# Softmax attention: row-sum reciprocals spread by a DRAM store and a repeating load, and four PSUM banks for transposes

## The reference, cut to what matters

```python
def one_block(args):                      # forgetting attention, 128 queries
    s = jnp.einsum('bhqd,bhkd->bhqk', qb, kh).astype(jnp.float32) * scale
    s = s + cb[..., :, None] - c[..., None, :]
    p = jax.nn.softmax(jnp.where(mask, s, -jnp.inf), axis=-1)
    return jnp.einsum('bhqk,bhkd->bhqd', p.astype(vh.dtype), vh)
...
def memory_attention(q, mk, mv):
    s = jnp.einsum('bthd,bmhd->bhtm', q, mk).astype(jnp.float32) * (D ** -0.5)
    p = jax.nn.softmax(s, axis=-1)
    o = jnp.einsum('bhtm,bmhd->bthd', p.astype(mv.dtype), mv)
...
o_fox = o_fox.astype(x.dtype) * jax.nn.silu(f_gate)
```

## Time and profile before

| | us |
|---|---|
| time before, median of 3 runs | 1407.98 (1406.86 to 1414.48) |
| profiled execution, its own time | 1410.44 |
| its span | 1408.6 |
| PE busy in the span | 1281.9 (91%) |
| DVE, ACT, POOL busy | 671.4, 547.2, 416.0 |
| memory attention | about 717 to 840 |
| forgetting attention | about 840 to 1217 |

### The profile page before, as it was taken

How to read it: one execution, slowest core, us unless ns; L and a number is a source line. 1 busy time by engine, 2 the same in 40 slices (tenths; PEclk the granted TensorE clock), 3 DMA queues, 4 the chain that set the end, 5 groups by cost and what they waited for, 6 DMA issues and landing times. The chain is left out here.

```text
span 1408.6 us, 20363 instructions
## 1 busy us (share of the span) xinstructions
PE 1281.9 (91%) x6624; PEld 1038.4 (74%) x6624; DVE 671.4 (48%) x1622; ACT 547.2 (39%) x1131; POOL 416.0 (30%) x464
## 2 busy tenths in 40 slices
PE   5898999999999999999976759998999999599997
PEld 4887867888777777788854546786777777478886
DVE  4564414200545544500045547887887888322222
ACT  3563214012222222211145646776777777310100
POOL 5222431021444444430005682223223412300000
PEclk9999999999999999999977888999999999799999
DMA  6454213222544454331156535134341611465453
GB/s 212 150 156 127 76 59 114 74 82 83 157 150 153 149 157 154 125 105 64 46 150 186 133 74 137 51 112 93 89 137 29 154 24 24 146 210 193 180 205 121
DMA packets 118350, 170.40 MB, mean 121 GB/s; under 512 B 11908, under 2 KB 74628, under 8 KB 116404
## 3 DMA queue, kind: packets, MB, share of 16 engines
q1 hardware_dynamic: 115768, 160.65, 37.9%
q10 hardware_dynamic: 2304, 8.39, 1.5%
q0 software_dynamic: 192, 0.33, 0.2%
HBM read 103.19 MB, written 66.13 MB: 120 GB/s over the span
## 5 line engine op out<-in xcount | busy, mean ns | idle before, releaser
L834 PE MATMUL cg_cps<-h_T,tok_slot 128*128 128x512 f32 x2112 | 493.7, 393 | 3.4 <-POOL tok_slot L1074 3.4
L834 PEld LDWEIGHTS cg_cps<-h_T,tok_slot 128*128 128x128 f32 x2112 | 396.4, 189 | 89.2 <-POOL tok_slot L1074 4.3
L1719 PE MATMUL out_yps<-out_w,out_mix 128*128 128x512 f32 x768 | 177.4, 393 | 18.3 <-DMA out_mix<-scr_mix 17.3
L1719 PEld LDWEIGHTS out_yps<-out_w,out_mix 128*128 128x128 f32 x768 | 145.8, 190 | 49.8 <-DMA out_mix<-scr_mix 17.5
L1559 DVE TENSOR_SCALAR_CACHE_REDUCE fox_prob<-fox_sps 128x512 f32<-128x512 f32 (+2 forms) x240 | 142.1, 607 | 37.8 <-PE fox_sps L1444 34.9
L1521 ACT ACTIVATE fox_pT<-fox_tps 128x512 fp32r<-128x512 f32 x240 | 124.6, 531 | 90.1 <-PE fox_tps L1454 87.6
L1570 DVE TENSOR_TENSOR fox_pT<-fox_tps,fox_pT 128x512 fp32r<-128x512 f32 x240 | 141.7, 605 | 21.6 <-ACT fox_pT L1521 20.9
L1454 PE MATMUL fox_tps<-all_ident,fox_prob 128*128 128x128 f32 x816 | 135.1, 278 | 15.4 <-ACT fox_prob L1513 8.5
L1467 PE MATMUL fox_ops<-fox_pT,fox_v 128*128 128x512 f32 x480 | 137.3, 376 | 0.0
L1454 PEld LDWEIGHTS fox_tps<-all_ident,fox_prob 128*128 128x128 f32 x816 | 100.4, 141 | 45.5 <-ACT fox_prob L1513 11.6
L1439 PE MATMUL fox_sps<-fox_ka,fox_qa 128*128 128x512 f32 (+2 forms) x240 | 107.4, 448 | 17.4 <-PEq L1376 14.0
(11 more groups left out here) (187 smaller groups left out, 1676.3 us busy)
## 6 DMA issues: line engine op xcount, KB each, us to landing
scr_split<-cg_stage SPq DMA_DIRECT2D x64, 256.0 KB, 2.8
out_mix<-scr_mix SPq DMA_DIRECT2D x32, 512.0 KB, 4.2
tok_xin<-in_w_cols SPq DMA_DIRECT2D x22, 512.0 KB, 4.4
tok_xin<-in_x SPq DMA_DIRECT2D x16, 512.0 KB, 3.9
scr_gates<-cg_stage SPq DMA_DIRECT2D x32, 256.0 KB, 2.4
out_x<-in_x SPq DMA_DIRECT2D x16, 512.0 KB, 6.1
out<-out_o ACTq DMA_DIRECT2D x16, 512.0 KB, 5.0
scr_fox_v<-tok_vst SPq DMA_DIRECT2D x16, 384.0 KB, 2.9
```

What stands on the lines that cost most here:

```text
L834: mm = nc.tensor.matmul(cps[u % 2][:, :], w[j % 2][a_][:, kk, :], hT[b_][:, kk, c * CH:(c + 1) * CH], start=(kk == 0 and r == 0), stop=(kk ...
L1719: mm = nc.tensor.matmul(yps[s][:, c, :], mix[s][a][:, kk, :], w[b][:, kk, c * CH:(c + 1) * CH], start=(kk == 0 and n == 0), stop=(kk == MI ...
```

## The change

The reciprocals no longer pass through PE and PSUM. After the first block of turn t, ACT issues a DMA that stores `rinv` to a DRAM row of 512 floats (`scr.inv`, one of two), each float to its own place in the order of the queries. SP then issues a load that reads this row 64 times, once for each partition of `scale`. ACT's store waits until the gate multiply of turn t - 2 is done, and so does SP's load; SP issues load_scale(t + 1) before it waits for the output of turn t, and the first, load_scale(0, 0), behind the list of first loads. The bank `rps` becomes a fourth `tps`, and PE's transposes may run one block further ahead of DVE. POOL's gate multiply waits for the load instead of ACT's copy. Its place in POOL's list stays.

```diff
@@ -55,6 +55,7 @@
         self.lr = dram("scr_lr", [GLA_R, T], F32)
         self.gla_b = dram("scr_gla_b", [64 + GLA_DK, 2, T], F32)
         self.crow = dram("scr_crow", [4, FOX_H, T], F32)
+        self.inv = dram("scr_inv", [2, CH], F32)
         self.mix = dram("scr_mix", [2, TT, P, MIX_T, P], F32)
 
 
@@ -1331,14 +1332,17 @@
         o = [k.sb(f"o{b}", [DH, CH]) for b in range(2)]
         om = [[k.sb(f"om{b}{i}", [DH, CH], F32R) for i in (HI, LO)] for b in range(2)]
         sps = [k.ps(f"sps{b}", [P, CH]) for b in range(2)]
-        tps = [k.ps(f"tps{b}", [P, CH]) for b in range(3)]
+        TPS = 4
+        tps = [k.ps(f"tps{b}", [P, CH]) for b in range(TPS)]
         ops = [k.ps(f"ops{b}", [P, CH]) for b in range(2)]
-        rps = k.ps("rps", [P, CH])
         names = ("pool_goes gate_scaled gate_loaded0 gate_loaded1 scored negated maxed expd transposed pt_hi pt_lo "
-                 "weighed inverted spread low_done added scaled gated o_hi o_lo stored0 stored1 sp_goes").split()
+                 "weighed inverted inv_stored0 inv_stored1 low_done added scale_loaded0 scale_loaded1 gated o_hi o_lo stored0 stored1 "
+                 "sp_goes act_goes").split()
         (pool_goes, gate_scaled, gate_loaded0, gate_loaded1, scored, negated, maxed, expd, transposed, pt_hi, pt_lo,
-         weighed, inverted, spread, low_done, added, scaled, gated, o_hi, o_lo, stored0, stored1, sp_goes) = map(k.sem, names)
+         weighed, inverted, inv_stored0, inv_stored1, low_done, added, scale_loaded0, scale_loaded1, gated, o_hi, o_lo, stored0,
+         stored1, sp_goes, act_goes) = map(k.sem, names)
         gate_loaded, stored = (gate_loaded0, gate_loaded1), (stored0, stored1)
+        scale_loaded, inv_stored = (scale_loaded0, scale_loaded1), (inv_stored0, inv_stored1)
 
         n_scores = sum(len(list(score_units(*t))) for t in turns)
         n_keys = sum(len(list(key_units(*t))) for t in turns)
@@ -1391,9 +1395,20 @@
                 for stage in next_stages:
                     stage.first_loads(sp)
 
+                def load_scale(r, t):
+                    b = t % 2
+                    sp.wait_ge(inv_stored[b], 16 * (r * (n_turns // 2) + t // 2 + 1))
+                    sp.sem_inc(sp_goes, 1)
+                    sp.wait_ge(gate_scaled, r * n_turns + max(t - 1, 0))
+                    sp.sem_inc(sp_goes, 1)
+                    sp.dma_start(scale[b][:, :], scr.inv[b].partition_broadcast(DH)).then_inc(scale_loaded[b], 16)
+
                 def round_(r, last):
                     for t, (e, g) in enumerate(turns):
-
+                        if t + 1 < n_turns:
+                            load_scale(r, t + 1)
+                        elif not last:
+                            load_scale(r + 1, 0)
 
                         sp.wait_ge(o_lo, r * n_turns + t + 1)
                         sp.sem_inc(sp_goes, 1)
@@ -1415,6 +1430,7 @@
                         if not last and t + 1 in (n_turns // 2, n_turns):
                             for piece in range(heads[e].pieces):
                                 heads[e].load_v(sp, r + 1, piece)
+                load_scale(0, 0)
                 rounds(sp, round_)
                 for b in range(2):
                     sp.wait_ge(stored[b], 16 * ROUNDS * n_turns)
@@ -1447,11 +1463,11 @@
 
                     def transposes(u, n, t, q0):
                         e, g, j, i0 = u
-                        pe.wait_ge(pt_lo, K.at(n - 2 if n >= 3 else 0))
+                        pe.wait_ge(pt_lo, K.at(max(n - TPS + 1, 0)))
                         for i in range(i0, QT):
                             if q0:
                                 pe.wait_ge(expd, E.at(QT * t + i + 1))
-                            mm = nc.tensor.transpose(tps[n % 3][:, i * P:(i + 1) * P],
+                            mm = nc.tensor.transpose(tps[n % TPS][:, i * P:(i + 1) * P],
                                                      prob[t % 2][:, i, j * P:(j + 1) * P], ident[:, :])
                         mm.then_inc(transposed, 1)
 
@@ -1468,16 +1484,6 @@
                                                   start=(first and i == HI), stop=(last and i == LO),
                                                   skip_group_check=True)
                         mm.then_inc(weighed, 1)
-
-                    def spread_sums(t):
-
-                        pe.wait_ge(inverted, G.at(t + 1))
-                        pe.wait_ge(scaled, G.at(t))
-                        for i in range(4):
-                            mm = nc.tensor.matmul(rps[0:DH, i * P:(i + 1) * P],
-                                                  rinv[t % 2][:, i:i + 1].to_broadcast([P, DH]), ident[:, :],
-                                                  start=True, stop=True)
-                        mm.then_inc(spread, 1)
 
                     if prologue:
                         for n, u in enumerate(score_units(*turns[0])):
@@ -1494,11 +1500,8 @@
                             waiting.append((u, k0 + m, t, m == 0, m == len(steps) - 1))
                             if len(waiting) > DEPTH:
                                 weigh(*waiting.pop(0))
-                            if ends(t, m):
-                                spread_sums(t - 1)
                     for x in waiting:
                         weigh(*x)
-                    spread_sums(n_turns - 1)
                 round_(0, False, prologue=True)
                 rounds(pe, round_)
 
@@ -1518,16 +1521,22 @@
                         e, g, j, i0 = u
                         act.wait_ge(transposed, K.at(n + 1))
                         act.wait_ge(weighed, K.at(max(n - PT + 1, 0)))
-                        nc.scalar.activation(pT[n % PT][HI][:, i0 * P:CH], tps[n % 3][:, i0 * P:CH], ACT.Copy
+                        nc.scalar.activation(pT[n % PT][HI][:, i0 * P:CH], tps[n % TPS][:, i0 * P:CH], ACT.Copy
                                              ).then_inc(pt_hi, 1)
 
                     def low_half(t):
                         act.wait_ge(weighed, K.at(at_turn(t + 1)[1]))
                         act.wait_ge(added, G.at(t))
                         nc.scalar.activation(low[:, :], ops[t % 2][DH:P, :], ACT.Copy).then_inc(low_done, 1)
-                        act.wait_ge(spread, G.at(t + 1))
-                        act.wait_ge(o_lo, G.at(max(t - 1, 0)))
-                        nc.scalar.activation(scale[t % 2][:, :], rps[0:DH, :], ACT.Copy).then_inc(scaled, 1)
+
+                    def store_inverses(t):
+                        b = t % 2
+                        act.wait_ge(inverted, G.at(t + 1))
+                        act.sem_inc(act_goes, 1)
+                        act.wait_ge(gate_scaled, G.at(max(t - 1, 0)))
+                        act.sem_inc(act_goes, 1)
+                        act.dma_start(scr.inv[b].rearrange("(i p) -> p i", p=P), rinv[b][:, :],
+                                      allow_slow_non_contiguous=True).then_inc(inv_stored[b], 16)
 
                     if prologue:
                         for i in range(QT):
@@ -1537,6 +1546,8 @@
                         k0 = at_turn(t)[1]
                         for m, (u, _, tiles) in enumerate(plan(t, last)[1]):
                             pt_high(u, k0 + m)
+                            if m == 0:
+                                store_inverses(t)
                             for i in tiles:
                                 exponentials(t + 1, i)
                             if ends(t, m):
@@ -1567,13 +1578,13 @@
                     def pt_low(u, n):
                         e, g, j, i0 = u
                         dve.wait_ge(pt_hi, K.at(n + 1))
-                        nc.vector.tensor_tensor(pT[n % PT][LO][:, i0 * P:CH], tps[n % 3][:, i0 * P:CH],
+                        nc.vector.tensor_tensor(pT[n % PT][LO][:, i0 * P:CH], tps[n % TPS][:, i0 * P:CH],
                                                 pT[n % PT][HI][:, i0 * P:CH].bitcast(F32), ALU.subtract
                                                 ).then_inc(pt_lo, 1)
 
                     def invert(t):
                         dve.wait_ge(expd, E.at(QT * (t + 1)))
-                        dve.wait_ge(spread, G.at(max(t - 1, 0)))
+                        dve.wait_ge(inv_stored[t % 2], 16 * (r * (n_turns // 2) + t // 2))
                         nc.vector.reciprocal(rinv[t % 2][:, :], rsum[t % 2][:, :]).then_inc(inverted, 1)
 
                     def add(t):
@@ -1613,7 +1624,7 @@
                     def gated_output(t):
                         b = t % 2
                         pool.wait_ge(gate_loaded[b], 16 * (r * (n_turns // 2) + t // 2 + 1))
-                        pool.wait_ge(scaled, G.at(t + 1))
+                        pool.wait_ge(scale_loaded[b], 16 * (r * (n_turns // 2) + t // 2 + 1))
                         nc.gpsimd.tensor_tensor(gate[b][:, :], scale[b][:, :], gate[b][:, :], ALU.mult
                                                 ).then_inc(gate_scaled, 1)
                         pool.wait_ge(gate_scaled, G.at(t + 1))
```

## The result

The changed kernel takes 1495.83 us (median of 4, 1493.68 to 1498.79), the kernel before beside it 1408.38 (1406.86 to 1414.48): ratio 1.0614, interval 1.0576 to 1.0651. It is slower by 6%; the forecast was 1395. The profiled execution took 1498.79 us, its span is 1497.1. In every run here the executions of one kernel agree within 0.6%, but for one of e2's eight, which took 2502.6 us and is left out of its ratio.

What follows compares the result with a forecast made beforehand. PE was taken to bound the forgetting stage, SP's issues and their order the memory stage. -24.7 and +11.1 sum to -13.6 us, giving 1396.8 from 1410.44 or 1394.4 from 1407.98: forecast 1395, range 1383 to 1411.

Steps and rivals of the forecast that it cites:

- the store's landing: Both attention stages: time for ACT's store of 512 single floats to land, taken as 2.5 us, bounds 2.0 and 4.4.
- In the forgetting stage both transfers are hidden: Forgetting stage: the store's 2.5 and the repeating load's 3.3 us are covered by a mean turn of 15.2 us.
- Rival (a): Memory stage: loses only 3 us because new waits replace old ones; 1386 us, chance 0.14.
- Rival (c): Memory stage: the store-and-load round trip sets the pace; 1405 us at landing 6.7 (chance 0.10), slower beyond 8.5 (0.08).
- The memory stage's +11.1: Memory stage: exposed transfers move POOL's last turn from 834.77 to 845.9, +11.1 us, bounds +3 and +21.
- the first two reasons: Memory stage, SP's order: first scale load behind bulk loads, turn 0 at 761; fifth behind next round's loads, turn 4 at 788.3.
- The forgetting stage's -24.7: Forgetting stage: sum of PE's cut, earlier end, fourth bank and DVE's share, -24.7 us, bounds -15 and -31.
- the fourth bank: Forgetting stage: a fourth transposes' bank spares PE waits for DVE to drain one, 3.4 us, bounds 0 and 6.7.
- -22.4 - 1.9 + 3.0: Forgetting stage: PE's spread removed in 22 turns, -22.4; stage's end starting earlier, -1.9; DVE limiting six turns, +3.0 us.
- the share that DVE takes back: Forgetting stage: in six turns where DVE is nearly the bound, half of PE's cut is lost, +3.0 us.

Runs made afterwards that it cites:

- e2: The changed kernel with each partition's four reciprocals stored side by side in DRAM, 128 packets of 16 bytes, scales in another order: 1406.42 us, ratio 0.9978.
- e3: The changed kernel with the stored floats 64 bytes apart in DRAM and the repeating load reading another row: 1405.72 us, ratio 0.9980.
- e13: The changed kernel with the stored floats 16 bytes apart in DRAM and the repeating load reading another row: 1415.2 us, ratio 1.004.
- e14: The changed kernel with the stored floats 8 bytes apart in DRAM and the repeating load reading another row: 1439.7 us, ratio 1.022.
- e4: The kernel before with the dense 512-float store added every turn, awaited only for buffer reuse four turns later and at the stage's end: 1465.48 us, ratio 1.0402.
- e6: The kernel before with the change in the forgetting stage alone, storing 16-byte runs, POOL reading the scale in matching order: 1387.42 us, ratio 0.9847.
- e11: e6 with three banks for transposes instead of four: 1397.07 us, ratio 0.9909 to the kernel before.
- e10: The changed kernel storing in partition order, floats 8 bytes apart in the partition so each stays a 4-byte packet into the same 2 KB: 1503.4 us, ratio 1.066.

## Why the prediction was wrong, point by point

**The step that failed is the store's landing**, the S that was taken at 2.5 us with bounds 2.0 and 4.4. It was 10. The bounds came from rows of stores with 384 runs of 512 bytes and of loads of 96 floats, and from the mean packet. None of these rows has many small writes close together, and the upper bound assumed that the cost of a packet is its time in the records. With the floats 64, 16 and 8 bytes apart the landings of 2.7, 3.1 and 4.3 us still lie within the bounds (e3, e13, e14); at the changed kernel's density the assumption fails. **A second effect had no term at all:** the store holds up other transfers, which alone costs 57 us in e4.

The Trainium skill ("DMA: Bandwidth & Descriptors", Rules for kernel authors, and Specifications) warned of one descriptor per element and of read-modify-write below 512 B. The direction was right, but neither alone makes the 10 us: e3's store has the same 512 packets of 4 bytes, and lands in 2.7 us, e13's in 3.1. Whether a read and write-back of bytes that neighbouring packets share makes the dense case slow, no run shows.

**"In the forgetting stage both transfers are hidden"** fell with it. The forecast set 5.8 us against the mean turn of 15.2. But 9.5 + 3.9 us is 13.4, and turns differ: e6's POOL starts its first three turns at 869.40, 874.53 and 883.76, that is, 5.1 and 9.2 us apart. The stage is 40.2 us longer than with e3's store: PE's busy time for the same 1872 instructions is 326.3 against 315.8 us, at a mean granted clock of 0.91 of full speed against 0.97 (10.5 us), and its idle time 62.2 against 32.5 (29.7 us).

**Rival (a)** fell with e3, whose memory stage loses 23.0 us even with a fast landing, and not 3. **Rival (c)** named the right loop, in the memory stage. With the measured landings its cycle is 0.4 + 10.3 + 5.0 + 1.3 = 17.0 us, 8.5 a turn, and POOL's turns 8 to 15 are (908.32 - 852.23) / 7 = 8.0 apart. Its price at S = 10 was 1425 and the time was 1496: it left out the loss in the forgetting stage (40.2 us) and the hold on other transfers, by which the repeating load itself took 5.0 us and not 3.3.

**The memory stage's +11.1 was mis-sized even with a good store**: e3 gives 866.2 - 843.2 = +23.0. By e3's starts on POOL against those forecast: turn 0 at 764.0 (761), turn 4 at 792.8 (788.3), turn 7 at 808.0 (802.6), turn 8 at 821.0 (810.9), turn 15 at 857.7 (845.9). The largest piece, 4.7 us, arises between turns 7 and 8, where the load's landing was 7.3 us and not 3.3; 3.0 arise at the start, 2.4 from turn 0 to 7, and 1.7 from a pace of 5.24 and not 5.0. The order on SP, the first two reasons, was right in kind: turn 2 is where ACT stops, and the fifth multiply waits.

**The forgetting stage's -24.7** held as a sum: -25.6 in e3, -24.2 in e6. Its terms did not. Without the fourth bank (e11) the stage is 14.2 us shorter, where -22.4 - 1.9 + 3.0 = -21.3 was forecast: PE's busy time fell by 341.9 - 320.4 = 21.5, as counted, but its idle time grew by 7.3 (32.0 to 39.3), with the wait for DVE's scaled scores up from 3.2 us to 9.4. So the share that DVE takes back was some 6, not 3, and e6's wait (8.5) shows that the fourth bank leaves it there. The bank gave 10.0 by the profile and 8.7, give or take 3, by the ratios, not 3.4; whether that is beyond the bound of 6.7, read from the wait for a free bank, is not settled. The idle time that went (6.3) agrees with that wait. The other 3.7 are in the lengths of matmul records, and where they come from is open. That the stage's sum came out right is luck: the bank gave more and DVE took more than forecast, and the two errors nearly cancel.

**The ledger** of the +88.5 us of span: +23.0 memory stage with a good store, -25.6 forgetting stage with a good store, +50.6 and +40.2 for the dense store in each, and 0.3 in the rest. The sum is 88.5. The first two cancel nearly, so even a store that lands as forecast gives e3's time, 1406, and not 1395.

## What to carry to other kernels

Before a tile is stored element by element, look at how densely its writes lie: set the small writes apart (64 bytes sufficed here), or let each partition write one run, and undo the order on the reading side. Time a transfer of a kind that the trace does not show by itself before bounding it by others. Where the same change falls into a stage paced by an engine and one paced by transfers, make it only in the first: that is e6, 1387 against 1408 us.

## What the runs showed of the hardware that was not expected

- 512 single-float writes from 128 partitions into 2 KB of DRAM land in 10 us, at 8, 16 and 64 bytes' distance in 4.3, 3.1 and 2.7 us; 128 writes of 16 bytes into the same 2 KB land in 2.4, and single-float reads as dense in 2.6.
- Such a store slows other transfers in flight: in e4, where none waits for it, output stores went from 2.5 to 4.9 us and forgetting gate loads from 3.1 to 5.8.
- The packets' records show none of this: 23424 packets and 2.3% of the engines' time in the changed kernel and in e3 alike.
- POOL's 64 x 512 multiply with one operand read at a distance of four floats took 1.5 us, against 1.26.
- An issue of 512 single floats holds ACT 0.37 us, close to its contiguous ones (0.34); with the floats 8 bytes apart in the partition (e10) it is 0.52.
